# Four decode tokens instead of eight in each block's scatter, and routing ahead of the row copies

## The reference

```python
def moe(h, router_w, router_bias, w_gate, w_up, w_down):
    ...
    scores = jax.nn.sigmoid((t @ router_w).astype(F32))
    sel = scores + router_bias.astype(F32)
    grp = lax.top_k(sel.reshape(-1, N_GROUPS, EXPERTS_PER_GROUP), TOP_K)[0].sum(-1)
    best = jnp.argmax(grp, axis=-1)
    ...
    for e in range(N_EXPERTS):
        he = jax.nn.silu(t @ w_gate[e]) * (t @ w_up[e])
        y = y + gates[:, e:e + 1] * (he @ w_down[e])
```

## Time and profile before

| what | value |
|---|---|
| time, median of 3 runs | 914.48 us (913.81 to 914.83) |
| the profiled execution: its time, its span | 914.91 us, 913.2 us |
| TensorE matmuls busy | 885.4 us, 97% of the span |
| VectorE, ScalarE busy | 378.7 us, 282.0 us |
| mean rate of HBM over the span | 327 GB/s |
| 40 slices: rate in slices 16 to 20 (layer 0's experts) | 425 to 428 GB/s |

### The profile page before, as it was taken

One profiled execution on the slowest core, in us unless ns is written; L12 is line 12 of the kernel. 1 busy time (PEld: TensorE's weight loads), 2 busy tenths in 40 slices (PEclk: granted clock), 3 DMA queues, 4 the chain that ended last, 5 costly groups with the idle time before them and its releaser, 6 DMA issues.

```text
span 913.2 us, 15657 instructions
## 1 busy us (share of the span) xinstructions
PE 885.4 (97%) x6503; PEld 552.7 (61%) x6503; DVE 378.7 (41%) x973; ACT 282.0 (31%) x597; POOL 102.8 (11%) x164
## 2 busy tenths in 40 slices
PE   9999999989999999999999998999999999999996
PEld 6878777767887344444425786777885343434424
DVE  1368877976314411111313335666337130211314
ACT  3524543322204220101003248788415120101013
POOL 2132040653000000000000101111400000000000
PEclk9999999999999999999999999999999999999998
DMA  9964254868998899999995884446699999999991
GB/s 374 352 242 173 106 191 177 319 245 344 420 431 332 352 383 429 427 428 427 425 425 245 360 378 146 142 146 243 239 425 403 418 388 427 427 427 427 426 407 55
DMA packets 26620, 299.77 MB, mean 328 GB/s; under 512 B 3432, under 2 KB 4968, under 8 KB 7080
## 3 DMA queue, kind: packets, MB, share of 16 engines
q1 hardware_dynamic: 21312, 268.51, 71.5%
q0 software_dynamic: 4544, 29.65, 8.9%
q10 hardware_dynamic: 688, 0.53, 0.2%
HBM read 283.26 MB, written 15.53 MB: 327 GB/s over the span
## 4 chain that ended last, share of the span: by engine, by line
PE 82%; DMA 9%; DVE 6%; ACT 1%; issue 1%; SPq 0%; POOL 0%; DVEq 0%; ACTq 0%; POOLq 0%
PE bank L1365 18%; PE bank L967 14%; PE bank L1389 11%; PE bank L1565 8%; PE bank L1214 6%; PE bank L1552 5%; DMA ring<-in_w_down 4%; DMA A<-in_w_down 4%; PE bank L1342 3%; PE bank L1235 3%; PE bank L1431 2%; PE bank L1403 2%; DMA ring<-in_w_ab 1%; PE bank L1026 1%; PE bank L1040 1%
## 5 line engine op out<-in xcount | busy, mean ns | idle before, releaser
L1365 PE MATMUL bank<-ring,W 128*32 128x512 f32 x1280 | 174.2, 593 | 0.4 <-DMA ring<-in_w_up 0.4
L967 PE MATMUL bank<-xT,ring 128*128 128x264 f32 x704 | 162.1, 388 | 0.9 <-DMA ring<-in_w_ab 0.9
L967 PEld LDWEIGHTS bank<-xT,ring 128*128 128x128 f32 x704 | 131.8, 190 | 28.2 <-issue 5.1
L1365 PEld LDWEIGHTS bank<-ring,W 128*32 128x32 f32 x1280 | 48.9, 110 | 98.8 <-issue 96.9
L1365 PE MATMUL bank<-A,W 128*32 128x512 f32 x512 | 98.5, 593 | 1.3 <-DMA ring<-in_w_up 1.3
L2605 DVE TENSOR_TENSOR gkg<-gkg,bank 128x512 f32<-128x512 f32 x16 | 11.0, 689 | 166.1 <-PE bank L1365 166.1
L1565 PE MATMUL bank<-xT,ring 128*128 128x264 f32 x320 | 76.1, 389 | 0.0
L1565 PEld LDWEIGHTS bank<-xT,ring 128*128 128x128 f32 x320 | 58.9, 190 | 10.2 <-issue 0.2
L1389 PE MATMUL bank<-A,W 128*32 128x512 f32 x352 | 63.1, 593 | 0.0
L1214 PE MATMUL bank<-A,ring 128*128 128x264 f32 x256 | 57.8, 387 | 0.3 <-ACT A L1651 0.3
L1389 PE MATMUL bank<-ring,W 128*32 128x512 f32 x416 | 56.3, 593 | 1.2 <-DMA ring<-in_w_down 1.2
(11 more groups left out here) (366 smaller groups left out, 1246.5 us busy)
## 6 DMA issues: line engine op xcount, KB each, us to landing
ring<-in_w_gate SPq DMA_DIRECT2D x21, 2048.0 KB, 17.9
ring<-in_w_up SPq DMA_DIRECT2D x18, 2048.0 KB, 17.4
ring<-in_w_down SPq DMA_DIRECT2D x13, 2048.0 KB, 20.4
ring<-in_w_ab SPq DMA_DIRECT2D x10, 2048.0 KB, 8.6
A<-in_w_down SPq DMA_DIRECT2D x10, 2048.0 KB, 16.9
A<-in_w_up SPq DMA_DIRECT2D x9, 2048.0 KB, 24.6
ring<-in_w_c SPq DMA_DIRECT2D x8, 2048.0 KB, 12.7
A<-in_w_gate SPq DMA_DIRECT2D x5, 2048.0 KB, 17.6
```

The lines of the kernel that those rows point to most:

```text
L967: mm = pe.matmul(ab_bank(m)[:, 0:T], slot(AB_IN0 + m // 4, 8)[:, c, (m % 4) * P:(m % 4 + 1) * P], xT[:, c, :], start=(c == 0), stop=(c == ...
L1365: mm = pe.matmul(out[ROWS * g:ROWS * (g + 1), :], xg[:, c, E_G * b + g, :], w[g][:, c % 4 // 2, c % 2, :], start=(c == 0), stop=(c == DC - 1))
```

## The change

Three edits. (1) `PT` becomes 132 columns wide: each block scatters its own four decode tokens only, and VectorE adds 4 columns for each chunk instead of 8. The decode half of `turn_weights` picks four of eight columns, so it is a matmul with a slice of the identity instead of a transpose. (2) In `route`, the two row copies and their wait move behind `sel` and the three sums, and the signal `row_roots` behind the six comparisons. (3) ScalarE's table load moves behind the four token copies. The edits hold for both layers.

```diff
-SPREAD_N = P + NB
+SPREAD_N = P + DCAP
...
                     for r in range(2 * QUADS):
-                        tr = pe.transpose(turned[r][:, P:SPREAD_N], WS2[:, r * P:(r + 1) * P], ident[0:NB, 0:NB])
+                        tr = pe.matmul(turned[r][:, P:SPREAD_N], WS2[:, r * P:(r + 1) * P],
+                                       ident[0:NB, DCAP * (r % 2):DCAP * (r % 2 + 1)], start=True, stop=True)
                     tr.then_inc(sem("pt_turned"), 1)
...
                 act.sem_inc(sem("moe_scores"), 1)
-                act.preload_act_table_set("silu_and_others")
                 for i in range(4):
...
+                act.preload_act_table_set("silu_and_others")
...
             def route(layer):
-                dve.wait_ge(sem("xtm_turned"), 6 * layer + 3)
-                st.add(dve.tensor_copy(row_roots, bank[3][:, P:3 * P].rearrange("p (b t) -> p b t", b=2)[:, :, 0]))
-                st.add(dve.tensor_copy(row_means_less, bank[1][:, P:3 * P].rearrange("p (b t) -> p b t", b=2)[:, :, 0]))
-                st.settle()
-                dve.sem_inc(sem("row_roots"), 1)
...
                     at += n
+                dve.wait_ge(sem("xtm_turned"), 6 * layer + 3)
+                st.add(dve.tensor_copy(row_roots, bank[3][:, P:3 * P].rearrange("p (b t) -> p b t", b=2)[:, :, 0]))
+                st.add(dve.tensor_copy(row_means_less, bank[1][:, P:3 * P].rearrange("p (b t) -> p b t", b=2)[:, :, 0]))
                 for gap in (1, 2, 3):
...
                 dve.wait_ge(st.sem, st.n - 6)
+                dve.sem_inc(sem("row_roots"), 1)
...
-                            for part, of in ((slice(P * b, P * (b + 1)), slice(0, P)), (slice(NP, T), slice(P, SPREAD_N))):
+                            for part, of in ((slice(P * b, P * (b + 1)), slice(0, P)),
+                                             (slice(NP + DCAP * b, NP + DCAP * (b + 1)), slice(P, SPREAD_N))):
```

## The result

The changed kernel took 917.38 us (median of 17 runs, 914.44 to 922.00) beside 914.59 for the kernel before (17 runs). The ratio is 1.0033 [1.0021, 1.0044]: 2.8 us slower, where 1.5 was forecast. The profiled execution took 919.56 us (span 917.7), so it shows more of the loss than the median.

What follows compares the result with a forecast made beforehand. TensorE's order was taken to bound most of the kernel, and the `w_down` stream each layer's expert end. A layer summed to -0.40 + 1.19 - 0.05 = +0.74 us; 914.48 + 1.5 gave 916.0 us, range 914.6 to 917.0.

Steps and rivals of the forecast that it cites:

- the price of `turn_weights`: Decode half of `turn_weights`, before the dip: sixteen matmul passes take 1.78 us in place of 0.59, losing 1.19 us a layer.
- what routing wins: Routing, before the dip: `sel` starts earlier, ahead of the row copies, gaining 0.40 us a layer, at most 0.47.
- the sum: A layer: -0.40 routing, +1.19 `turn_weights`, -0.05 tail, so +0.74 us; two layers +1.5 us.
- the same dip: In each layer's weight stream: DMA engines run dry until SyncE's two issues; down to 98 GB/s in layer 0, 49 in layer 1.
- rivals 2 and 3: `turn_weights` passes: 2, a matmul costs four transposes, 917.1 us, chance 0.07; 3, 74 ns each, 914.8 us, chance 0.08.
- Tail: Last quad's scatter, after the last weights: four narrower VectorE adds save 0.05 us a layer.
- Token copies and table load: ScalarE in routing: copies end at 292.3, before the gather; the moved table load hides behind the gather and costs nothing.
- Rival 1: Routing: `row_roots` comes late, the gather waits for the token copies, the gain is lost; 916.8 us, chance 0.10.
- One for one: TensorE's time before the dip moves the refill, the stream's end and the layer's end by the same amount.
- Rival 4: Weight stream: it has unseen slack that absorbs all before the dip; only the tail is left, 914.4 us, chance 0.10.

Runs made afterwards that it cites:

- f4: f4_busy_norm: e3_transposed plus one unused matmul of 264 columns in TensorE's wait for the norm, ahead of routing; 912.61 us, 0.9980 of before.
- j5: j5_look: the changed kernel with no edit, one more profiled execution; 914.79 us.
- e0: e0_before: the kernel before run again, no edit; median 914.56 us, 1.0001 of before.
- j4: j4_look: the changed kernel with no edit, one profiled execution; 916.41 us.
- h3: h3_before_busy: the kernel before plus f4's unused matmul of 264 columns; 914.10 us, 0.9993 of before.
- h1_wide: e3_transposed plus two unused matmuls of 512 and 264 columns (1.31 us) behind `turn_weights`; 916.35 us, 1.0020 of before.
- f1: f1_after_again: the changed kernel run again on chip 0, no edit; 917.39 us, 1.0035 of before.
- e1: e1_scatter_only: the kernel before with edit 1 alone, routing and table load as before; 917.81 us, 1.0031 of before.
- j3: j3_4_first: the changed kernel with the passes ahead of the prompt transposes, still 4 columns each; 917.27 us, 1.0027 of before.
- f2: f2_spread: the changed kernel with the eight decode matmuls one by one between the matmuls of the up pass; 917.92 us, 1.0037 of before.
- f3: f3_doubled: the changed kernel with the sixteen passes issued twice; 924.69 us, 1.0113 of before.
- h4: h4_two_groups: the changed kernel with eight passes behind the prompt transposes, eight behind the first half of up; 917.10 us, 1.0032 of before.
- j1: j1_116_columns: the changed kernel with the passes ahead of the prompt transposes, 116 columns each; 917.26 us, 1.0029 of before.
- e2: e2_route_only: the kernel before with edits 2 and 3 alone, scatter and transposes as before; 914.72 us, 0.9995 of before.
- e3: e3_transposed: the changed kernel with the decode half made by 8-column transposes ahead of the prompt transposes; 913.85 us, 0.9992 of before.
- h2: h2_after_busy: the changed kernel plus f4's unused matmul of 264 columns; 915.87 us, 1.0017 of before.

## Why the prediction was wrong

The sign was right, and the two terms that decide it: the price of `turn_weights` is more than what routing wins. The size was not, since TensorE's clock has a part in it that the sum left out.

**The step that failed** is the sum: "two layers, with the same shapes and the same dip: +1.5 us". Every term in it came from one execution in which TensorE ran at full clock, and there was no term, and no rival, for a change of the clock: it was put at nothing without a reason. In the changed kernel 9 of 17 executions have a mean clock of 0.994 or less, and took 917.24 us or more (median 919.50); the eight others took 914.44 to 917.38 (median 915.54). The first profile shows two places. Routing: a fall takes the gain of 0.47 away and adds 0.94. Behind the passes: 1.70 us. With f4's matmul in both kernels, and no fall seen in routing, the change costs 1.8 to 2.2 us, without it 2.8 to 3.0. So some 1 us of the loss may be what the falls in routing cost the changed kernel more than the kernel before; that is an estimate, and no larger than the error of such a difference. The executions without any fall until the end can't price the change by their times: 914.79 us changed (j5), 913.85 (e0) and 914.91 before. By the table's stretches j5 loses 0.6 to 0.8 us to those two, all in layer 1. So the full-clock sum of +1.5 was rather too high, for the reason given below under "one for one", and that the median came out only 1.4 us above the forecast is in part luck.

**The terms at full clock.** Routing: 0.47 instead of 0.40, at the upper bound that the dummy matmuls set. The passes: 1.28 instead of 1.19; a pass takes 0.117 us, not 0.111, inside the bounds, so rivals 2 and 3 are out. The figure of the Trainium skill (TensorE: Matmul & The Clock Gate, Terms), a transpose four times faster for fp32, is near the trace here: 0.235 us a matmul against 0.074, 3.2 times. Tail: layer 0 from the landing of `w_down` to the end of the sums of the last squares (L1267) takes 22.05 us instead of 22.10, the 0.05 that was forecast.

**Token copies and table load, "at nothing"**: right. The copies start at 288.81, earlier than forecast, and end at 291.60; the gather starts at 293.99 and doesn't wait for them (in j5 they end at 291.68, the gather starts at 292.66). Rival 1's loss of the routing gain did come, but through TensorE and not through the copies.

**"One for one" before the dip**: borne out in layer 1. From before to j5 the landing moves by 0.84 us there, and -0.47 + 1.28 = +0.81. j4 with its fall is 1.78 later than j5, for 1.70. But single landings vary: in h3, the kernel before with f4's matmul, the last `w_down` of layer 1 lands 198.75 us behind the last residual matmul, 1.42 later than before, with no fall until then. In layer 0 it was wrong. The refill moves as forecast (in j5 SyncE's second issue comes at 338.88, or 56.19 us behind the last residual matmul, before 55.38: 0.81 later), but the landing doesn't: j4 and j5 land 0.07 to 0.27 us **earlier** than before, where +0.81 was due. The last `w_down` too is issued later, 162.77 us behind the last residual matmul instead of 162.16 (0.47 less, 1.28 more, 0.20 less for two scatters), but it lands 35.18 us after its issue instead of 36.06 (35.87 in e0). Rival 4 had a part of the truth there. In layer 0 this transfer takes 35.18 to 35.43 us in all eleven profiles with the new matmuls, and 35.62 to 36.31 in the seven without, h1_wide with its 36.31 among them, which has the same time in another form and does move the landing one for one. Why the thin passes don't stays open.

**What stays open.** The falls are more frequent with sixteen passes of 4 columns in a row: 0.994 or less in 23 of 51 executions (the changed kernel, f1, e1, j3), against 14 of 108 of the kernel before. Part of that is the place behind the passes, where 3 of 14 layers profiled with such a row show a fall, all in layer 1. But routing seems to have them more often too: 7 of 12 layers profiled in such kernels without the unused matmul (8 of 20 with f2, f3, h4 and j1, which have the passes in other forms), against 1 of 10 in before, e0, e2, e3 and h1. In layer 0 no new matmul stands ahead of routing, so this can't be the passes of that layer; it may be chance, since falls come together in single executions. No run settles it, nor why the clock falls in one execution and not in the next.

## What to carry to other kernels

Replacing a transpose by a small fp32 matmul saves columns and costs passes: count passes, at a price from a row that has such a matmul. Ask of each stretch of TensorE that a sum rests on what it takes at half clock, and profile more than one execution: the same kernel's profile took 914.79 us in one and 919.56 in another. An off-path gain that ends against TensorE's own work (here four dummy matmuls) is gone as soon as that work runs at half speed.

## What the runs showed of the hardware

- TensorE's granted clock fell from 2.4 to 1.2 GHz in the same instructions in some executions and not in others. In routing it fell as tokens were turned, as the granted clock of 0.50 from 288 us on shows. Three falls came behind waits of TensorE: of 1.94 us in e3's first mixer, of 2.08 and 2.03 us for weights in layer 1 of f4 and h2. The Trainium skill (TensorE: Matmul & The Clock Gate, Part 4: PE-mode transpose) says that full clock doesn't engage for transposes; the traces don't bear that out as a rule, since j5 turns the same tokens at full clock (1.31 us for 12, and 2.56 at half clock in the first profile).
- With one unused matmul of 264 columns in the wait ahead of routing (f4, h2, h3) none of the six layers profiled has a fall in routing, and none of 35 executions a mean clock of 0.994 or less; of the changed kernel without it, 13 of 28 have (its first runs and f1).
- Thin 8-row passes between the matmuls of the up pass cost 1.25 us a layer more than in a row (f2, at full clock).
- A pass with 8 rows takes 0.117 us with 4 columns and 0.123 with 116.
